# Expert down products in plain 32 bit instead of split, rounded operands

## What is computed

```python
def hier_moe(h, w_r1, b_r1, w_r2, b_r2, w_g, w_u, w_d):
    ...
    y = jnp.zeros((B * S, Dm), jnp.float32)
    for e in range(N_EXPERTS):
        a = jax.nn.silu(x @ w_g[e]) * (x @ w_u[e])
        y = y + gate[:, e:e + 1] * (a @ w_d[e]).astype(jnp.float32)
    return y.astype(h.dtype).reshape(B, S, Dm)
```

## Time and profile before

| what | value |
|---|---|
| median of three runs | 1157.56 us (1153.74 to 1158.6) |
| span of the profiled execution, first to last instruction | 1142.0 us |
| own device time of the profiled execution | not listed apart; the runs lie 11.7 to 16.6 us above its span |
| PE busy | 1083.6 us (95%) |
| DVE busy | 402.0 us (35%) |
| ACT busy | 283.7 us (25%) |
| mean granted TensorE clock | 0.910 |
| experts, first gate product to last down product | some 471 to 1110 us |

### The profile page before, as it was taken

One profiled execution on the slowest core, in us unless ns is written; L12 is line 12 of the kernel. 1 busy time (PEld: TensorE's weight loads), 2 busy tenths in 40 slices (PEclk: granted clock), 3 DMA queues, 4 the chain that ended last, 5 costly groups with the idle time before them and its releaser, 6 DMA issues.

```text
span 1142.0 us, 16399 instructions
## 1 busy us (share of the span) xinstructions
PE 1083.6 (95%) x6668; PEld 882.8 (77%) x6668; DVE 402.0 (35%) x745; ACT 283.7 (25%) x485; POOL 84.8 (7%) x156
## 2 busy tenths in 40 slices
PE   6999999999999999989999999999999999999980
PEld 4666666456546655789999999999999999999970
DVE  1014440065312053314343525243433434252533
ACT  3013220023502133112222323131313222231321
POOL 2010000010100001400000000000000000000004
PEclk9996559965699998979999999999999999999995
DMA  8926003230204423278989899999989898988804
GB/s 238 385 96 258 1 1 111 74 120 1 74 1 161 171 74 139 91 260 321 361 340 352 337 353 340 350 354 342 370 331 365 336 357 336 355 339 324 290 11 147
DMA packets 54354, 264.56 MB, mean 232 GB/s; under 512 B 10648, under 2 KB 10672, under 8 KB 45712
## 3 DMA queue, kind: packets, MB, share of 16 engines
q1 hardware_dynamic: 46016, 236.18, 55.5%
q0 software_dynamic: 5600, 19.51, 5.5%
q10 hardware_dynamic: 2704, 8.39, 2.0%
HBM read 249.33 MB, written 16.58 MB: 233 GB/s over the span
## 4 chain that ended last, share of the span: by engine, by line
PE 91%; DVE 3%; DMA 3%; issue 1%; POOL 1%; ACT 1%; ACTq 0%; SPq 0%; POOLq 0%; DVEq 0%
PE pA L1151 39%; PE pS L1165 11%; PE pA L882 10%; PE pA L875 9%; PE pS L915 5%; PE pA L949 5%; PE pTr L1142 3%; PE pTr L930 2%; PE pA L857 2%; PE pTr L866 1%; PE pS L919 1%; DMA zone<-hn_d,idx_cur 1%; DMA zone<-y_d,slot 1%; POOL slot_d L592 1%; PE pA L1102 0%
## 5 line engine op out<-in xcount | busy, mean ns | idle before, releaser
L1151 PEld LDWEIGHTS pA<-zone,ring 128*128 128x128 f32 x4096 | 473.5, 194 | 4.6 <-issue 0.5
L1151 PE MATMUL pA<-zone,ring 128*128 128x64 f32 x4096 | 470.8, 276 | 0.0
L1487 DVE TENSOR_TENSOR zone<-zone,pS 64x1024 f32<-64x1024 f32 x32 | 38.8, 1212 | 349.2 <-ACT zone L774 349.2
L1482 DVE TENSOR_TENSOR w_lo<-ring,w_hi 128x1024 fp32r<-128x1024 f32 x128 | 150.5, 1218 | 19.8 <-ACT w_hi L761 19.8
L761 ACT ACTIVATE w_hi<-ring 128x1024 fp32r<-128x1024 f32 x128 | 127.7, 1046 | 30.5 <-DVE zone L1487 30.5
L774 ACT ACTIVATE zone<-pS 64x1024 f32<-64x1024 f32 x32 | 32.7, 1021 | 393.2 <-PE pS L1165 393.2
L882 PE MATMUL pA<-ring,hT 128*128 128x512 f32 (+1 forms) x240 | 106.3, 601 | 1.0 <-DVE hT L1236 1.0
L1165 PE MATMUL pS<-w_hi,a_split 128*128 128x512 f32 x256 | 104.1, 407 | 0.0
L1165 PE MATMUL pS<-w_lo,a_split 128*128 128x512 f32 x256 | 100.8, 394 | 0.0
L875 PE MATMUL pA<-hT,ring 128*128 128x320 f32 x320 | 91.1, 448 | 0.5 <-DVE hT L1236 0.5
L882 PEld LDWEIGHTS pA<-ring,hT 128*128 128x128 f32 (+1 forms) x240 | 41.3, 175 | 61.5 <-issue 60.9
(11 more groups left out here) (195 smaller groups left out, 732.4 us busy)
## 6 DMA issues: line engine op xcount, KB each, us to landing
ring<-in_w_exp_gate SPq DMA_DIRECT2D x32, 2048.0 KB, 10.6
ring<-in_w_exp_up SPq DMA_DIRECT2D x32, 2048.0 KB, 8.7
ring<-in_w_exp_down SPq DMA_DIRECT2D x32, 2048.0 KB, 13.9
ring<-in_w_in SPq DMA_DIRECT2D x6, 2048.0 KB, 21.4
y_d<-zone ACTq DMA_DIRECT2D x32, 256.0 KB, 5.0
ring<-in_w_out SPq DMA_DIRECT2D x2, 2048.0 KB, 18.4
ring<-in_w_ck SPq DMA_DIRECT2D x1, 2048.0 KB, 25.6
ring<-in_w_cv SPq DMA_DIRECT2D x1, 2048.0 KB, 7.7
```

The costliest lines, as they stand in the source:

```text
L1151: last = mm(pA[b][:, x * GW + f * SLOTS:x * GW + (f + 1) * SLOTS], w[:, c, f * P:(f + 1) * P], xeT[:, b, c, :], start=c == 0, stop=c == C - 1)
L1482: nv.tensor_tensor(w_lo[:, f, :], by_k(3 * b + 2, FC)[:, f, :], w_hi[:, f, :].bitcast(F32), ALU.subtract).then_inc(w_lo_ready, 1)
L1487: nv.tensor_tensor(ysb[:, b, :], ysb[:, b, :], pS[b][0:SLOTS, :], ALU.add).then_inc(y_summed, 1)
```

## The change

The down product takes `aT` and the ring slot as they are, in plain 32 bit: 4 chunks x 2 halves, one matmul each, 64 stationary columns, output on partitions 0 to 63. `w_hi`, `w_lo`, `a_split` and the steps that fill them are gone. ACT evicts the left half of the result and DVE the right half, both straight into `ysb`. A down slot of the ring counts as read when the down product that read it is done (`y_ready`). PE itself waits for the load of the down slot. The final gain `gfin` lies in another buffer. Gate and up products are unchanged.

```diff
@@ expert_weights (SP)
                 if first:
                     sp.wait_ge(a_ready, a_done[RING + s])
-                elif n < 2:
-                    sp.wait_ge((gate_read, gu_ready)[n], r * NE + e - 1)
                 else:
-                    sp.wait_ge(w_lo_ready, (r * NE + e - 1) * FC)
+                    sp.wait_ge((gate_read, gu_ready, y_ready)[n], r * NE + e - 1)
...
@@ ACT
-            def split(b, chunks):
-
-                for f in chunks:
-                    act.activation(w_hi[:, f, :], by_k(3 * b + 2, FC)[:, f, :], ACT.Copy).then_inc(w_hi_ready, 1)
-
...
-                act.activation(ysb[:, b, :], pS[b][SLOTS:2 * SLOTS, :], ACT.Copy).then_inc(y_lower, 1)
+                act.activation(ysb[:, b, 0:512], pS[b][0:SLOTS, 0:512], ACT.Copy).then_inc(y_left, 1)
 
             def rows_out(n, b, r, e):
 
-                act.wait_ge(y_summed, n + 1)
+                act.wait_ge(y_left, n + 1)
+                act.wait_ge(y_right, n + 1)
...
                 n = r * NE + e
-                lower_rows(n - 1, 1 - b, first_out)
-                act.wait_ge(w_in_s[3 * b + 2], (n - b) * 8 + 48)
-                split(b, (0,))
+                left_rows(n - 1, 1 - b, first_out)
                 rows_out(n - 1, 1 - b, r, e - 1)
-                split(b, range(1, FC))
                 sigmoid(n, b, first)
...
@@ PE
             def down(n, b, first=False):
 
                 pe.wait_ge(at_ready, n + 1)
+                pe.wait_ge(w_in_s[3 * b + 2], (n - b) * 8 + 48)
                 if not first:
-                    pe.wait_ge(y_summed, n - 1)
+                    pe.wait_ge(y_left, n - 1)
+                    pe.wait_ge(y_right, n - 1)
+                w = by_k(3 * b + 2, FC)
                 for f in range(FC):
-                    a = a_split[:, b, f, :, :].rearrange("p k s -> p (k s)")
-                    pe.wait_ge(w_lo_ready, n * FC + f + 1)
                     for half in range(2):
-                        for part in (w_hi, w_lo):
-                            last = mm(pS[b][0:2 * SLOTS, half * 512:(half + 1) * 512], a, part[:, f, half * 512:(half + 1) * 512],
-                                      start=f == 0 and part is w_hi, stop=f == FC - 1 and part is w_lo)
+                        last = mm(pS[b][0:SLOTS, half * 512:(half + 1) * 512], aT[:, b, f * SLOTS:(f + 1) * SLOTS],
+                                  w[:, f, half * 512:(half + 1) * 512], start=f == 0, stop=f == FC - 1)
                 last.then_inc(y_ready, 1)
...
@@ DVE
-                nv.tensor_tensor(aT[:, b, :], sg[:, b, :], pA[b][:, GW:2 * GW], ALU.mult).then_inc(a_split_step, 1)
-                dve.wait_ge(a_split_step, n * 3 + 2)
                 if not first:
                     dve.wait_ge(y_ready, n - 1)
-                a = aT[:, b, :].rearrange("p (f s) -> p f s", f=FC)
-                nv.tensor_copy(a_split[:, b, :, 0, :], a).then_inc(a_split_step, 1)
-                dve.wait_ge(a_split_step, n * 3 + 3)
-                nv.tensor_tensor(a_split[:, b, :, 1, :], a, a_split[:, b, :, 0, :].bitcast(F32), ALU.subtract).then_inc(at_ready, 1)
+                nv.tensor_tensor(aT[:, b, :], sg[:, b, :], pA[b][:, GW:2 * GW], ALU.mult).then_inc(at_ready, 1)
                 rows_in(n + 2, b)
 
-            def lower_weights(n, b):
-
-                for f in range(FC):
-                    dve.wait_ge(w_hi_ready, n * FC + f + 1)
-                    nv.tensor_tensor(w_lo[:, f, :], by_k(3 * b + 2, FC)[:, f, :], w_hi[:, f, :].bitcast(F32), ALU.subtract).then_inc(w_lo_ready, 1)
-
-            def sum_rows(n, b):
-
-                dve.wait_ge(y_lower, n + 1)
-                nv.tensor_tensor(ysb[:, b, :], ysb[:, b, :], pS[b][0:SLOTS, :], ALU.add).then_inc(y_summed, 1)
+            def right_rows(n, b, first=False):
+
+                dve.wait_ge(y_ready, n + 1)
+                if not first:
+                    dve.wait_ge(y_stored[b], (n - b) * 8)
+                nv.tensor_copy(ysb[:, b, 512:1024], pS[b][0:SLOTS, 512:1024]).then_inc(y_right, 1)
...
```

More of the change, by code:

```diff
@@ L125, in build @@
         ygat = zone[:, 0:6144].rearrange("p (t k d) -> p t k d", t=TILES, k=2)
-        gfin = zone[:, 6144:7168]
         ident = sb("ident", [P, P])
@@ L208, in build @@
         hankel = oall[:, 0:2, :].rearrange("p t (h j) -> p (t h) j", j=256)
+        gfin = ktok[:, :, :].rearrange("p t w -> p (t w)")[:, 0:D]
         qxT = relb[:, :, :].rearrange("p h k -> p (h k)")[:, 0:M4 * NTOK].rearrange("p (m t) -> p m t", m=M4)
-        w_hi = sb("w_hi", [P, FC, D], F32R)
-        w_lo = sb("w_lo", [P, FC, D], F32R)
-        a_split = sb("a_split", [P, 2, FC, 2, SLOTS], F32R)
         pA = [ctx.enter_context(nc.psum_tensor(f"pA{b}", [P, 512], F32)) for b in range(2)]
@@ L299, in build @@
         y_ready = sem("y_ready")
[L300 to L304, removed]
+        gated = sem("gated")
+        y_left = sem("y_left")
+        y_right = sem("y_right")
         y_stored = [sem(f"y_stored{b}") for b in range(2)]
@@ L767, in sigmoid, with left_rows @@
                 act.activation(sg[:, b, :], pA[b][:, 0:GW], ACT.Sigmoid).then_inc(sig_ready, 1)
-            def lower_rows(n, b, first=False):
+            def left_rows(n, b, first=False):
                 act.wait_ge(y_ready, n + 1)
@@ L801, in experts @@
                 n = r * NE
-                act.wait_ge(w_in_s[2], n * 8 + 48)
-                split(0, range(FC))
                 first = isinstance(r, int)
@@ L812, in experts @@
                 n += NE - 1
-                lower_rows(n, 1)
+                left_rows(n, 1)
                 rows_out(n, 1, r, NE - 1)
@@ L1465, in activations, with expert @@
                 dve.wait_ge(sig_ready, n + 1)
-                nv.tensor_tensor(sg[:, b, :], sg[:, b, :], pA[b][:, 0:GW], ALU.mult).then_inc(a_split_step, 1)
-                dve.wait_ge(a_split_step, n * 3 + 1)
-                nv.tensor_tensor(aT[:, b, :], sg[:, b, :], pA[b][:, GW:2 * GW], ALU.mult).then_inc(a_split_step, 1)
-                dve.wait_ge(a_split_step, n * 3 + 2)
+                nv.tensor_tensor(sg[:, b, :], sg[:, b, :], pA[b][:, 0:GW], ALU.mult).then_inc(gated, 1)
+                dve.wait_ge(gated, n + 1)
                 if not first:
                     dve.wait_ge(y_ready, n - 1)
-                a = aT[:, b, :].rearrange("p (f s) -> p f s", f=FC)
-                nv.tensor_copy(a_split[:, b, :, 0, :], a).then_inc(a_split_step, 1)
-                dve.wait_ge(a_split_step, n * 3 + 3)
-                nv.tensor_tensor(a_split[:, b, :, 1, :], a, a_split[:, b, :, 0, :].bitcast(F32), ALU.subtract).then_inc(at_ready, 1)
+                nv.tensor_tensor(aT[:, b, :], sg[:, b, :], pA[b][:, GW:2 * GW], ALU.mult).then_inc(at_ready, 1)
                 rows_in(n + 2, b)
-            def lower_weights(n, b):
-                for f in range(FC):
-                    dve.wait_ge(w_hi_ready, n * FC + f + 1)
-                    nv.tensor_tensor(w_lo[:, f, :], by_k(3 * b + 2, FC)[:, f, :], w_hi[:, f, :].bitcast(F32), ALU.subtract).then_inc(w_lo_ready, 1)
-            def sum_rows(n, b):
-                dve.wait_ge(y_lower, n + 1)
-                nv.tensor_tensor(ysb[:, b, :], ysb[:, b, :], pS[b][0:SLOTS, :], ALU.add).then_inc(y_summed, 1)
-            def expert(n, b, first=False):
-                sum_rows(n - 1, 1 - b)
-                lower_weights(n, b)
+            def right_rows(n, b, first=False):
[3 more added lines that the diff above has]
+                nv.tensor_copy(ysb[:, b, 512:1024], pS[b][0:SLOTS, 512:1024]).then_inc(y_right, 1)
+            def expert(n, b, first=False, first_out=False):
+                right_rows(n - 1, 1 - b, first_out)
                 activations(n, b, first)
@@ L1496, in experts @@
                 first = isinstance(r, int)
-                lower_weights(n, 0)
                 if first:
@@ L1501, in experts @@
                 activations(n, 0, first)
-                expert(n + 1, 1, first)
-                with dve.Fori(1, NE // 2) as p:
+                expert(n + 1, 1, first, first)
+                expert(n + 2, 0, False, first)
+                expert(n + 3, 1)
+                with dve.Fori(2, NE // 2) as p:
                     for b in range(2):
                         expert(n + p * 2 + b, b)
-                sum_rows(n + NE - 1, 1)
+                right_rows(n + NE - 1, 1)
             experts(0)
```

## The result

The changed kernel took 1253.82 us in the median of four runs (1243.48 to 1264.16), the kernel before 1155.65 us in four runs beside it. The ratio is 1.0837, with a 95% interval from 1.0772 to 1.0903: slower by 8.4%. The ratio leaves out the run of 1264.16 us, which counts as slow because it lies over 1.5% above the fastest. The forecast was 1261 us, with a range of 1250 to 1270 us. The profiled execution took 1251.22 us, and its span is 1249.5 us, so only 1.7 us lie around the span.

A forecast was written before the change was run, and what follows sets the result against it. PE was taken to bound the expert loop. Thirty down products at +3.28 us, the first +3.4 and the last +3.3 gave +105.1 us; less 1.55 at the end, +103.6 on 1157.56 made 1261 us, range 1250 to 1270.

The forecast's parts named there:

- PE is the bound, the splits are covered: In the expert loop time is PE time; removing splits of 150.5 us DVE and 127.7 us ACT gives nothing.
- The price of a plain record from line 882: Cross-attention output product of the same shape: 0.438 us a record, so each down product goes from 3.73 to 7.01 us.
- The first rival: Down product: each plain matmul costs four rounded records, 7.46 us per down product, 1276 us in all; 4%.
- The weight load at the change of products: From down to up product, a 194 ns load could be exposed: taken as 0, 6 us at most.
- The first down product and the end: First down product, partly at low clock, +3.4 us to 8.2 us; side-by-side eviction at the end gives 1.55 us back.
- SP's queue and the DMA engines: Down load issued 15.8 us after the up load, gate load behind it, at no cost; DMA share falls to 0.76.
- The base: Time around the span taken as unchanged, so the increase was added to 1157.56 us, 15.6 us above the 1142.0 us span.
- The start: 471 to 504 us: clock drop after PE's wait for gathered rows; its absence would gain 7.9 us, kept for the low end.
- The clock did not fall in the loop: Rival in the expert loop: one product per expert at the lower clock, 6.75 us each, 1477 us; 3%.
- the gate load came in time: Rival in SP's queue: gate load late behind the down load's wait, 10.1 us per expert, 1584 us; 4% on the contrary case's sibling: 2%.
- the matmul did not go through as one record: Rival in the down product: a plain matmul is one record, 3.50 us per down product, 1149 us; 2%.
- the DMA engines did not set the pace: Rival in the loop: DMA, not PE, sets the 19.56 us, so the change is hidden, 1156 us; 2%.

The follow-up runs named there:

- the wide operand: Changed kernel with the down product's stationary operand widened from 64 to 128 columns, the added ones zeros; two runs of 1254.66 and 1257.05 us.
- the fillers: More 512-column filling matmuls at the experts' start: on the kernel before 1138.66 us, on the changed kernel 1249.88 us.
- the kernel with the gate load first: Changed kernel with the next expert's gate load issued ahead of this expert's down load in SP's order; 1258.87 and 1263.14 us.

## Why the prediction was right, and where not

**PE is the bound, the splits are covered.** Right, and shown: the distance is the same with and without the splits. DVE lost 186 us where about 150 were forecast and ACT 138 where 128 were, since the activation steps and part of the eviction went as well; nobody waited for them.

**The price of a plain record from line 882.** Right: 7.01 us forecast and measured, 16 records, clock 1.00. This one row of the same shape carried 98.4 of the 103.6 us that were forecast. The first rival, four rounded records for a plain matmul at 7.46 us, is out: 16 records of full width took 6.92 us, 0.865 us a matmul, 3.7 times the rounded record's 0.233. At 2.4 GHz a plain record's 0.43 us is some 1030 cycles for 512 columns (an estimate from the two chains above), twice 512, and a matmul has two records. The Trainium skill's four passes (FP8 and Floating Point Precision, TensorE Precision Notes) fit this trace as a count, by that estimate; as a price in rounded records they come out 6 to 8% high.

**The weight load at the change of products, taken as 0.** Wrong in size: the sum had 0 with 6 us kept for the range, and it was 0.20 us x 31 = 6.2 us. The reason given, that the loads of line 882 run beside its matmuls, said nothing about the load that follows them. The row that did say it was in the trace: the third gate product of the kernel before, directly behind transposes, stands in the chain as

```profile
516.93 7.29 PE pA L1151 x64
```

and its neighbours as 7.09. What the wide operand shows is that the width matters. The Trainium skill (TensorE: Matmul & The Clock Gate, Step-by-step: what each phase is for) says that PE pulls weight loads ahead of matmuls in flight, when the row groups do not conflict or the load goes to the background buffer. Here the load stands ahead between products of full width (0.43 us ahead with the wide operand) and not from a 64-column product, nor from the 64-row transposes, to one of 128 x 128; why was not tried.

**The first down product and the end.** Right for this execution: 8.02 us against 8.2, and the store issued 0.8 us after the last matmul against 0.75. Where the clock fell earlier the first down product took 8.79 us, with the fillers 7.01. (The lower rows that ACT copied in the kernel before are partitions 64 to 127; DVE added 0 to 63.)

```profile
1219.27 0.59 ACT L760 ACTIVATE zone<-pS 64x512 f32<-64x512 f32 x1 [10.42 <-PE pS L1147]
1219.27 0.68 DVE L1460 COPY zone<-pS 64x512 f32<-64x512 f32 x1 [8.92 <-PE pS L1147]
1220.04 0.49 ACTq L773 DMA_DIRECT2D y_d<-zone  x1
```

**SP's queue and the DMA engines.** Right: the issue times came as worked out (down load 15.8 us after the up load, at 579.00 after 563.25, gate load behind it), the share fell to 0.77 (forecast 0.76), and moving the gate load changed nothing in the loop.

**The base.** Wrong: "I take what lies around the span as unchanged" put 15.6 us between span and time. It is 1.7 us, and 1.7 to 1.9 us in the other runs of the kernel before, whose spans run from 1139.6 to 1156.0. So the span of 1142.0 us belonged to an execution at the low end of the scatter, and the medians to others. The increase, 103.6 us, was 4 us too small against the profiled spans (the 6.2 us, less 1.7 us at the start and some tenths elsewhere), and the base it was added to was the median of three runs of a kernel that scatters by 16 us. The medians differ by 98.2 us, the profiled spans by 107.5 and the two kernels with fillers by 109.2, so that the mix of starts alone is worth more than the error. That the time came out only 7 us below the forecast is in part luck: for the profiled execution the same sum gives 1142.0 + 103.6 + 1.7 = 1247.3 us, below the range, where 1251.22 was measured.

**The start.** Half right: the fall of the clock behind the wait for gathered rows was seen, and kept as a possible gain of 7.9 us. That it can also fall before the first product, and then costs 13 us more, was not thought of. It is the larger part of the scatter. The changed kernel's runs fit this: 1243.48 us is 7.7 us below the profiled run, as without either fall, and 1264.16 us is 12.9 us above it, as with both; no trace of these two runs exists, so it is a fit and not shown.

**The rivals.** None took place. The clock did not fall in the loop, in the two traces of the kernel before without its filler either; the down product did not reach 7.46 us, the gate load came in time, the matmul did not go through as one record, and the DMA engines did not set the pace even at 17.74 us.

## What to carry to other kernels

Price a change of number format by a row of the same shape in the same trace, in time per listed record and with the count of records per matmul: here 16 rounded records and 16 plain ones differed by 3.28 us, and the work saved on two engines for which nobody waited was worth nothing. When operand widths change, price the first weight load behind the change as well, by the places where products of unlike shape already meet. Before adding a difference to a median, find out which execution the profile shows; here a scatter of 16 us in 1150 came mostly from the start of the experts, where the clock fell earlier in some executions than in others, and eight more filling matmuls there took 14 us off the median.

## What the runs showed of the hardware

- In the kernel with the gate load first, PE ran gate and up products (64 moving columns, a 128-column load for each record) for 27.00 of 27.00 us from 472 to 499 us at a granted clock of 0.50. The clock rose during the first down product, which has 512 moving columns (0.80 on average over its 8.79 us), and was 1.00 in the loop. In the kernel before without the filler in its loop, the same gate and up products ran at 1.00 for 559 us with a down product every 19.13 us. With the additional fillers of 512 columns at the start, the clock was 1.00 from 470 us on in both kernels.
- A gate or up product (128-column loads) behind a 64-column down product or behind transposes of 64 rows takes 7.29 us; behind the filler or a 128-column down product it takes 7.09.
- The DMA engines kept up 380 GB/s at a share of 1.00 for 502 us without PE waiting once.
